# A two-layer hybrid encoder on one core: six weight slots around the projections, splits and copies placed elsewhere

## The reference, cut to what matters

```python
for l in range(2):
    mix = hybrid_mixer(rmsnorm(h, norm_mix_pre[l]), w_in[l], ..., w_out[l])
    h = h + rmsnorm(mix, norm_mix_post[l])
    ff = square(relu(rmsnorm(h, norm_mlp_pre[l]) @ w_mlp_up[l])) @ w_mlp_down[l]
    h = h + rmsnorm(ff, norm_mlp_post[l])
# hybrid_mixer: z = h @ w_in, split into x, gate, q, k, v, g_out, zg
#   RG-LRU group: conv of x, two gated scans (forward, backward), times gelu(gate)
#   GLA group: chunked gated linear attention over q, k, v, both ways, per-head norm, times silu(g_out)
#   concatenate([y_lru, y_gla]) @ w_out
```

## Time and profile before

| | us |
|---|---|
| median of three runs (lowest, highest) | 2449.21 (2448.45, 2449.9) |
| time of the profiled execution | 2447.89 |
| its span, first to last instruction | 2446.1 |
| TensorE busy in the span | 2379.8 |
| GpSimd busy in the span | 751.4 |
| VectorE busy in the span | 1006.9 |

### The profile page before, as it was taken

The page is one execution under the profiler, slowest core; times in us unless marked ns, Lnnn a source line. Parts: engine busy times, 40 slices in busy tenths (PEclk is TensorE's granted clock), DMA queues, the critical chain, the costliest instruction groups (busy, mean ns, idle before and its releaser), DMA issues.

```text
span 2446.1 us, 35177 instructions
## 1 busy us (share of the span) xinstructions
PE 2379.8 (97%) x15144; PEld 2308.1 (94%) x15144; DVE 1006.9 (41%) x989; ACT 585.3 (24%) x719; POOL 751.4 (31%) x401
## 2 busy tenths in 40 slices
PE   7999999999999999999899999999999999999996
PEld 6999989899999999999889998898999999999996
DVE  5688543731221221221577974528221222222226
ACT  4464332321011011011336452414110110110012
POOL 3333213323233233233413421142332332333331
PEclk9999999999999999999999999999999999999998
DMA  3011001511111111111231110015111111111123
GB/s 137 22 56 35 27 27 52 150 52 44 52 43 43 51 43 43 51 60 47 89 113 44 36 43 27 21 63 161 35 53 43 43 51 43 44 50 43 46 76 113
DMA packets 57642, 139.02 MB, mean 57 GB/s; under 512 B 4944, under 2 KB 32848, under 8 KB 57552
## 3 DMA queue, kind: packets, MB, share of 16 engines
q1 hardware_dynamic: 28368, 99.20, 12.4%
q10 hardware_dynamic: 29184, 38.49, 5.0%
HBM read 120.57 MB, written 17.10 MB: 56 GB/s over the span
## 4 chain that ended last, share of the span: by engine, by line
PE 90%; DVE 5%; ACT 2%; issue 1%; POOL 1%; DMA 0%; ACTq 0%; DVEq 0%; SPq 0%; POOLq 0%
PE banks L416 78%; PE banks L517 2%; PE banks L460 2%; DVE Y L1181 1%; PE banks L449 1%; DVE acc L1134 1%; PE banks L450 1%; PE banks L463 1%; PE banks L662 1%; PE banks L669 1%; PE banks L618 1%; PE banks L639 1%; POOL w_hl L348 1%; DVE Y L1191 1%; PE banks L740 1%
## 5 line engine op out<-in xcount | busy, mean ns | idle before, releaser
L416 PE MATMUL banks<-X,w_hl 128*128 128x348 f32 (+1 forms) x7776 | 1263.0, 323 | 6.7 <-POOL w_hl L348 4.8
L416 PEld LDWEIGHTS banks<-X,w_hl 128*128 128x128 f32 x7776 | 1237.9, 188 | 16.1 <-issue 13.2
L346 POOL TENSOR_SCALAR w_hl<-w_raw 128x1024 fp32r<-128x1024 f32 x176 | 200.7, 1140 | 1559.7 <-PE banks L416 1109.9
L416 PE MATMUL banks<-act_hi,w_hl 128*128 128x348 f32 (+1 forms) x2880 | 537.2, 321 | 0.0
L348 POOL TENSOR_TENSOR w_hl<-w_raw,w_hl 128x1024 fp32r<-128x1024 f32 x176 | 497.5, 2827 | 14.7
L416 PEld LDWEIGHTS banks<-act_hi,w_hl 128*128 128x128 f32 x2880 | 471.2, 188 | 0.0
L1080 ACT ACTIVATE T<-T 128x1044 f32<-128x1044 f32 x64 | 69.1, 1079 | 1196.5 <-DVE T L1526 1196.5
L1526 DVE SCALAR_TENSOR_TENSOR T<-banks,rs 128x1044 f32<-128x1044 f32 x64 | 79.7, 1245 | 583.8 <-PE banks L416 573.6
L416 PE MATMUL banks<-act_lo,w_hl 128*128 128x348 f32 (+1 forms) x1440 | 306.4, 321 | 0.0
L1547 DVE TENSOR_TENSOR Y<-banks,Y 128x1044 f32<-128x1044 f32 x96 | 119.5, 1245 | 374.4 <-PE banks L416 374.4
L416 PEld LDWEIGHTS banks<-act_lo,w_hl 128*128 128x128 f32 x1440 | 241.3, 188 | 0.0
(11 more groups left out here) (159 smaller groups left out, 1836.4 us busy)
## 6 DMA issues: line engine op xcount, KB each, us to landing
w_raw<-w_units SPq DMA_DIRECT2D x184, 512.0 KB, 3.4
h_mid<-Y ACTq DMA_DIRECT2D x24, 348.0 KB, 4.2
h_out<-Y ACTq DMA_DIRECT2D x24, 348.0 KB, 2.5
Y<-x_in ACTq DMA_DIRECT2D x6, 696.0 KB, 9.8
h_old<-x_in ACTq DMA_DIRECT2D x12, 348.0 KB, 3.7
h_old<-h_mid ACTq DMA_DIRECT2D x12, 348.0 KB, 3.5
h_old<-h_out ACTq DMA_DIRECT2D x12, 348.0 KB, 3.6
X<-h_mid ACTq DMA_DIRECT2D x6, 696.0 KB, 9.2
```

Of the source, the lines that this page charges most:

```text
L346: nc.gpsimd.tensor_scalar(slot[:, 0], w_raw[:, s], 1.0, 1.0, ALU.mult, ALU.mult).then_inc(w_rounded, 1)
L416: ins = nc.tensor.matmul(out[:, b, 0:width(b)], wp, xp[:, used(b)], start=first and n == 0, stop=last and n == 2)
```

## The change

There are two more slots, 4 and 5 (w_out0 and w_out1), laid over the tiles of gg (A_YL), which are also those of act_hi. The units around the projections go to other slots and are split at other points of GpSimd's order:

- The first pair of each layer goes to slots 0 and 1 instead of 3 and 2. In layer 1 its second unit is split only after the squares of block 0 have been added (acc_done). The layer's units 2 and 3 are split after the jobs of gate 0 and x 0 rather than at once, and the first gate weights between them without a wait for x 0.
- U_OUT+2 and +3 go to slots 4 and 5, after the last `lru_lo` (x_lo) and J_SG[3]; +4 and +5 to slots 0 and 1, +6 and +7 to slots 2 and 3, all after J_O+1.
- U_MLP and U_MLP+1 go to slots 4 and 5 after J_O+2 and J_O+3; U_MLP+2 after J_O+4; U_MLP+3 after J_O+5 and the end of the update (x_lo).
- The last two down units go to slots 2 and 3, with no slot to wait for.
- ScalarE copies v rows 0 and 1 before `decay_exps(0)`, and the later copies are shifted by one; in `update` the norm's `log_mean` and `inv_root` of block 2 stand before `new_piece(5)` instead of after it.

```diff
--- before.py
+++ after.py
@@ -195,6 +195,7 @@
         h_old = at("h_old", [128, 3, 2, BN], A_D)
         w_third = at("w_third", [128, 2, 8, 128], A_D + 2, f32r)
         w_fourth = at("w_fourth", [128, 2, 8, 128], A_T + 3, f32r)
+        w_out = [at("w_out0", [128, 2, 8, 128], A_YL, f32r), at("w_out1", [128, 2, 8, 128], A_YL + 2, f32r)]
         late_sq = (T[0], at("late_sq", [128, NP], A_END))
         sq = at("sq", [128, SQ_RING, 2, BN], A_T + 1)
         Y = at("Y", [128, KT, NP], A_QK)
@@ -202,7 +203,7 @@
         act_lo = at("act_lo", [128, GT, NP], A_SG, f32r)
         assert 4 * 2 * 4 * 128 <= TB and 4 * NC * HEADS * DV <= 5 * TB and 4 * NC * 4 * DV <= 5 * TB
-        wslots = (w_hl[:, 0], w_hl[:, 1], w_third, w_fourth)
+        wslots = (w_hl[:, 0], w_hl[:, 1], w_third, w_fourth, *w_out)
         banks = ctx.enter_context(nc.psum_tensor("banks", [128, 8, 512], f32))
@@ -351,6 +352,11 @@
                 for s, before in ((0, before0), (1, before1)):
                     split(l, i, s, before, wslots[slots[s]])
+            def ups(l, g):
+                i0 = U_MLP // 2 + 4 * g
+                split_pair(l, i0, done(l, j_down(g - 1, 5)), done(l, j_down(g - 1, 7)))
+                split_pair(l, i0 + 1, done(l, j_up(g, 0)), done(l, j_up(g, 1)))
             def downs(l, g, before0, before1):
                 i0 = U_MLP // 2 + 4 * g
                 split_pair(l, i0 + 2, before0, before1)
@@ -359,7 +365,7 @@
             def split_gates(l, t):
                 pool.wait_ge(gatew_loaded, 16 * (l * LT + t + 1))
-                pool.wait_ge(mm_done, FIRST + done(l, j_lru(t - 1, 3) if t > 0 else j_x(0)))
+                pool.wait_ge(mm_done, FIRST + (done(l, j_lru(t - 1, 3)) if t > 0 else l * NJ))
                 pool.sem_inc(waited_pool, 1)
                 nc.gpsimd.tensor_scalar(gates_hl[:, 0], gates_raw[:, :, :], 1.0, 1.0, ALU.mult, ALU.mult).then_inc(gates_hi, 1)
                 pool.wait_ge(gates_hi, l * LT + t + 1)
@@ -368,17 +374,21 @@
             for l in range(L):
-                free = done(l - 1, j_up(0, 1)) if l > 0 else 0
-                split_pair(l, 0, free, free, (3, 2))
+                if l > 0:
+                    split(l, 0, 0, done(l - 1, j_down(GROUPS - 1, 1)), wslots[0])
+                    pool.wait_ge(acc_done, count(ADDS, l - 1, 1) + KT - 1)
+                    split(l, 0, 1, done(l - 1, j_down(GROUPS - 1, 3)), wslots[1])
+                else:
+                    split_pair(l, 0, 0, 0)
                 pool.wait_ge(zgw_loaded, 16 * (l + 1))
                 pool.sem_inc(waited_pool, 1)
                 nc.gpsimd.tensor_scalar(zg_hl[:, :, 0], zg_raw[:, :, :], 1.0, 1.0, ALU.mult, ALU.mult).then_inc(zgw_step, 1)
                 pool.wait_ge(zgw_step, l + 1)
                 nc.gpsimd.tensor_tensor(zg_hl[:, :, 1], zg_raw[:, :, :], zg_hl[:, :, 0].bitcast(f32), ALU.subtract)\
                     .then_inc(zgw_ready, 1)
-                split(l, 1, 0, l * NJ, wslots[1])
-                split(l, 1, 1, l * NJ, wslots[0])
+                split(l, 1, 0, done(l, j_gate(0)), wslots[1])
                 split_gates(l, 0)
+                split(l, 1, 1, done(l, j_x(0)), wslots[0])
                 split(l, 2, 0, done(l, j_v(0)), wslots[1])
                 split_gates(l, 1)
                 split(l, 2, 1, done(l, j_x(1)), wslots[0])
@@ -395,16 +405,23 @@
                 split_pair(l, 8, done(l, J_K[0]), done(l, J_K[1]), (1, 0))
                 split_pair(l, 9, done(l, J_SG[0]), done(l, J_SG[1]), (1, 0))
                 split_pair(l, U_OUT // 2, done(l, J_SG[2]), done(l, J_SG[3]), (1, 0))
-                with pool.Fori(1, 4) as i:
-                    split_pair(l, U_OUT // 2 + i, done(l, J_O - 2 + 2 * i), done(l, J_O - 1 + 2 * i), (1, 0))
-                split_pair(l, U_MLP // 2, done(l, J_O + 1), done(l, J_O + 1), (3, 2))
-                split_pair(l, U_MLP // 2 + 1, done(l, J_O + 7), done(l, J_O + 7))
+                pool.wait_ge(x_lo, l * X_PER + NX + LT)
+                split_pair(l, U_OUT // 2 + 1, done(l, J_SG[3]), done(l, J_SG[3]), (4, 5))
+                split_pair(l, U_OUT // 2 + 2, done(l, J_O + 1), done(l, J_O))
+                split_pair(l, U_OUT // 2 + 3, done(l, J_O + 1), done(l, J_O + 1), (2, 3))
+                split_pair(l, U_MLP // 2, done(l, J_O + 2), done(l, J_O + 3), (4, 5))
+                split(l, U_MLP // 2 + 1, 0, done(l, J_O + 4), wslots[0])
+                pool.wait_ge(x_lo, l * X_PER + NX + LT + HEADS + NX)
+                split(l, U_MLP // 2 + 1, 1, done(l, J_O + 5), wslots[1])
                 downs(l, 0, done(l, j_up(0, 2)), done(l, j_up(0, 3)))
-                with pool.Fori(1, GROUPS) as g:
-                    i0 = U_MLP // 2 + 4 * g
-                    split_pair(l, i0, done(l, j_down(g - 1, 5)), done(l, j_down(g - 1, 7)))
-                    split_pair(l, i0 + 1, done(l, j_up(g, 0)), done(l, j_up(g, 1)))
+                with pool.Fori(1, GROUPS - 1) as g:
+                    ups(l, g)
                     downs(l, g, done(l, j_up(g, 2)), done(l, j_up(g, 3)))
+                g = GROUPS - 1
+                ups(l, g)
+                split_pair(l, U_MLP // 2 + 4 * g + 2, done(l, j_up(g, 2)), done(l, j_up(g, 3)))
+                split_pair(l, U_MLP // 2 + 4 * g + 3, done(l, J_O + 6), done(l, J_O + 7), (2, 3))
         @block.tensor
@@ -450,17 +467,17 @@
                 nc.tensor.matmul(sum_bank(norm, b), ones[:, :], sq[:, n % SQ_RING, 1, :], start=False, stop=last)\
                     .then_inc(sum_done if last else sq_read, 1)
-            def first_pair(l, norm, unit, j, xbase, sbase, last_sum):
+            def first_pair(l, norm, unit, j, slots, xbase, sbase, last_sum):
                 def hi_passes(u, b, k):
-                    w = wslot((3, 2)[u], k)
+                    w = wslot(slots[u], k)
                     for n, wp in enumerate(w):
                         nc.tensor.matmul(ps(j + u)[:, b, 0:width(b)], wp, xtile(k)[0][:, used(b)], start=k == 0 and n == 0, stop=False)
                 def lo_pass(u, b, k):
-                    return nc.tensor.matmul(ps(j + u)[:, b, 0:width(b)], wslot((3, 2)[u], k)[0], xtile(k)[1][:, used(b)],
+                    return nc.tensor.matmul(ps(j + u)[:, b, 0:width(b)], wslot(slots[u], k)[0], xtile(k)[1][:, used(b)],
                                             start=False, stop=k == KT - 1)
                 for n in range(NX):
@@ -729,7 +746,7 @@
             for l in range(L):
                 xbase = l * X_PER
-                first_pair(l, PRE_MIX, 0, j_x(0), xbase, l * 2 * NX, (l - 1, 1, NB - 1) if l > 0 else None)
+                first_pair(l, PRE_MIX, 0, j_x(0), (0, 1), xbase, l * 2 * NX, (l - 1, 1, NB - 1) if l > 0 else None)
                 pe.wait_ge(zgw_ready, l + 1)
                 take_set(l, J_ZG)
@@ -755,12 +772,11 @@
                 unit_with(l, U_K, J_K[0], {3 + n: [rows[n]] for n in range(5)})
                 unit_with(l, U_K + 1, J_K[1], {n: [rows[5 + n]] for n in range(7)})
                 gla(l, xbase)
-                with pe.Fori(1, 3) as i:
-                    unit_job(l, U_OUT + 2 * i, 1, J_O, J_O // 2 + i)
-                    unit_job(l, U_OUT + 2 * i + 1, 0, J_O + 1, (J_O + 1) // 2 + i)
-                by_blocks(l, 0, (U_OUT + 6, U_OUT + 7), (1, 0), [xtile(k) for k in range(KT)], {(1, 0, 5): 0, (2, 1, 6): 1})
-                first_pair(l, PRE_MLP, U_MLP, J_MLP, xbase + NX + LT + HEADS, l * 2 * NX + NX, (l, 0, NB - 1))
+                for m, s in ((2, 4), (3, 5), (4, 0), (5, 1)):
+                    unit_job(l, U_OUT + m, s, J_O + m, (J_O + m) // 2)
+                by_blocks(l, 0, (U_OUT + 6, U_OUT + 7), (2, 3), [xtile(k) for k in range(KT)], {(1, 0, 5): 0, (2, 1, 6): 1})
+                first_pair(l, PRE_MLP, U_MLP, J_MLP, (4, 5), xbase + NX + LT + HEADS, l * 2 * NX + NX, (l, 0, NB - 1))
                 unit_job(l, U_MLP + 2, 0, J_MLP + 2, (J_MLP + 2) // 2)
                 unit_job(l, U_MLP + 3, 1, J_MLP + 3, (J_MLP + 3) // 2)
                 for i in range(4):
@@ -775,7 +791,7 @@
                     unit_job(l, U_MLP + 8 * g + i, i % 2, j_up(g, i), j_up(g, i) // 2)
                 for i in range(2):
                     down_unit(l, g, i)
-                by_blocks(l, 1, (U_MLP + 8 * g + 6, U_MLP + 8 * g + 7), (0, 1), [(act_hi[:, k, :], act_lo[:, k, :]) for k in range(GT)],
+                by_blocks(l, 1, (U_MLP + 8 * g + 6, U_MLP + 8 * g + 7), (2, 3), [(act_hi[:, k, :], act_lo[:, k, :]) for k in range(GT)],
                           {(1, 1, 2): 0, (2, 3, 2): 1})
                 if l == L - 1:
                     row_sum(l, 1, NB - 1)
@@ -877,9 +893,9 @@
                         new_piece(n)
                 else:
                     new_piece(4)
-                    new_piece(5)
                     log_mean(l, norm, 2)
                     inv_root(l, norm, 2)
+                    new_piece(5)
                     new_piece(6)
                     log_mean(l, norm + 1, 0)
                     for n in range(7, NX - 1):
@@ -978,12 +994,13 @@
```

(7 more changed lines are left out.)

## The result

| | before | after |
|---|---|---|
| median, us | 2449.49 (4 runs, 2448.45 to 2449.9) | 2414.76 (4 runs, 2413.53 to 2415.16) |
| profiled execution, us | 2447.89 | 2414.39 |
| its span, us | 2446.1 | 2412.6 |

The median before now has a fourth run in it. The ratio is 0.9862, 95% interval 0.985 to 0.9874: 34.7 us less. The forecast was 2419 with a range from 2411 to 2431.

The account below looks back on a forecast made before the run. TensorE, busy 2379.8 of 2446.1 us, bounds the kernel, so only its waits can be won: ceiling 38.1 us with the clock, less 1.3, 1.4, 3.7 and 1.7, gives 30.0. Forecast 2419 us, range 2411 to 2431.

Parts of the forecast that it names:

- v rows: ScalarE's v copies ahead of the exponentials: TensorE's wait goes, 5.6 us less 1.3, gain 4.3.
- The 0.65 us that it kept for group 8: v rows: TensorE wants group 8 at about 252.0, group 6's copy ends about 252.6; 0.65 us lost per layer.
- Output projection: U_OUT+2 split in front: 8.5 us of waits and clock won, 1.4 lost at head 0; gain 7.1.
- The hidden 0.16: At each listed wait of TensorE: the recorded wait hides 0.16 us more; 17 waits, 2.7 us.
- The head wait of 0.7: Low part of head 0: GpSimd's second subtraction delays the normalisation, a new TensorE wait of 0.7 us per layer.
- The second rival: Head chain at the output projection: turns cost more, 6.3 us a layer instead of 0.7, 2430; chance 0.15.
- by_blocks and first_pair after the mixer: Unit waits in by_blocks, mixer row sums and waits inside first_pair go; two layers gain 9.6 us.
- The reading of the 1.6 us: Inside first_pair: wait follows from VectorE's scalings held by splits of U_MLP+2 and +3; ScalarE's earlier log_mean helps.
- Between the layers: Start of layer 1: TensorE still waits 3.4 us in two parts, slow stretch of 1.7 stays; 5.4 kept in all.
- the hold of VectorE: Between the layers: layer 1's second unit's split and zg make VectorE's scaling wait 1.4 us, its adds 1.3.
- The wait of 1.1 us at the row sum of block 1: Between the layers: a TensorE wait of 1.1 us, beside about 2.3 for the last emptying.
- Layer start: GpSimd's splits beside the convolution delay it 7.5 or 9 us, under the 11 in hand: costs nothing.

Follow-up runs that it names:

- e1_v_old: Changed kernel with only ScalarE's v row copies put back behind the first exponentials; 2421.0 us, ratio 0.9886.
- experiment 2: Four kernels around the 1.6 us first_pair wait: ScalarE's log_mean order and GpSimd's MLP splits undone singly and together, the former alone on the kernel before; 2414.26, 2415.03, 2420.32, 2445.01 us.
- e5_head_free: Changed kernel with U_OUT+3 split only after the last low part of a head; 2413.81 us, ratio 0.9859.
- e3_split_back: Changed kernel with U_MLP+2 and +3 split together behind J_O+7, as before; 2415.03 us, ratio 0.9863.
- e10: Changed kernel with VectorE emptying the last two parts of by_blocks before new_piece(2), between the layers only; 2415.43 us, ratio 0.9865.
- e12: Changed kernel with U_OUT+3 split later, no squares wait, and, between the layers, banks emptied and ScalarE's log_mean and inv_root moved before new_piece(2); 2409.66 us, ratio 0.9841.
- e15_before_log: Kernel before with only log_mean and inv_root of block 2 moved ahead of new_piece(5) on ScalarE; 2445.01 us, ratio 0.9986.
- e4_out_late: Changed kernel with U_OUT+2 and +3 still in slots 4 and 5 but split only after J_O and J_O+1; 2419.12 us, ratio 0.9881.
- e2: Changed kernel with only log_mean and inv_root of block 2 back behind new_piece(5) on ScalarE; 2414.26 us, ratio 0.9857.
- e9: Changed kernel with both ScalarE's log_mean order and the splits of U_MLP+2 and +3 put back as before; 2420.32 us, ratio 0.9884.
- e14: The changed kernel once more, unedited, on the same chip in five rounds; 2414.26 us, ratio 0.9858.
- e6_no_acc_wait: Changed kernel without GpSimd's wait for block 0's squares ahead of layer 1's second unit; 2412.26 us, ratio 0.9852.
- e13_two_waits: Changed kernel with U_OUT+3 split behind the heads and no wait for the squares before layer 1's second unit; 2411.41 us, ratio 0.9849.

## Why the prediction was right, and where it was off

**Sign, size and places** held: 34.7 us measured, 30 forecast, and nearly every wait went or came where the prediction had put it. The forecast lay 4.2 us above the median, which is in its range but 0.2 us under the band, 2415 to 2424, to which it gave most of its chance. Of the miss 3.5 us are in the steps; the rest is that the changed kernel's profiled execution lay only 0.4 below its median, where the prediction had added the 1.3 of the kernel before. Its terms, in its own order:

- **v rows.** The mechanism held: e1_v_old brings the 5.3 us back. The 0.65 us that it kept for group 8 was 0.25 in each layer. VectorE's products were held as it said (two took 5.36 us from 244.33), but the copies of groups 6 to 8 started at 250.70, so group 6's end, put at 252.6, came at 251.3.
- **Output projection.** The waits went and the clock stayed up. Of each step of 4.0 us 2.4 are the wait and 1.6 the clock, where 2.55 and 1.7 were forecast. The hidden 0.16 was not won here, since the changed kernel too takes 0.32 us from start to start where it goes over to U_OUT+2. The clock's part is a dozen matmuls that start 0.29 us apart, from 389.07 on, and 0.16 in the changed kernel. The head wait of 0.7 came as 0.4. The second rival, 6.3 us a layer, did not come: U_OUT+3's raw unit was there, and the second subtraction ended at 366.36.
- **by_blocks and first_pair after the mixer.** 9.6 forecast, 10.1 measured; the last units gave 4.7 and not 4.2. The reading of the 1.6 us was incomplete: it named VectorE as the cause and ScalarE's order as a help, and experiment 2 shows that the wait needs both of them, so that changing either is enough. The other reading would have given the same forecast, so the total could not tell: here the number was right without the mechanism being known.
- **Between the layers.** Measured 5.6, forecast 4.8. The term that was mis-sized is the hold of VectorE: 1.2 us at the scaling and 0.5 at the additions, where 1.4 and 1.3 were forecast. The wait of 1.1 us at the row sum of block 1 did not come: TensorE asked at 1199.01 and the squares had been added at 1198.74. The whole shortage showed at the bank set, 2.3 us as forecast, with its slow stretch, as forecast.
- **Layer start.** "Nothing" held for the time, and here the rows decide what was left open. The convolution in layer 0, VectorE, then GpSimd:

```profile
54.44 2.94 DVE L1332 TENSOR_SCALAR xc<-xb,par 128x1044 f32<-128x1044 f32 x1
57.42 5.80 DVE L1336 SCALAR_TENSOR_TENSOR xc<-xb,par,xc 128x1044 f32<-128x1044 f32 x3
63.26 2.78 DVE L1343 CAST xc_hl<-xc 128x1044 fp32r<-128x1044 f32 x1
```

```profile
54.43 2.40 POOL L349 TENSOR_TENSOR w_hl<-w_raw,w_hl 128x1024 fp32r<-128x1024 f32 x1
57.95 2.17 POOL L372 TENSOR_TENSOR gates_hl<-gates_raw,gates_hl 128x512 fp32r<-128x512 f32 x1
62.21 3.26 POOL L349 TENSOR_TENSOR w_hl<-w_raw,w_hl 128x1024 fp32r<-128x1024 f32 x1
```

In the trace before, the same three lines took 0.81, 3.99 and 0.70 us. The first and the last have one operand in SBUF, and both wait for GpSimd's subtraction as those with two do. By this the rule that the prediction cited from the Trainium skill (GPSIMD Engine Reference, 1. Specifications), that VectorE's two-port modes contend too, agrees with the trace; in which mode the two lines ran, no row here shows. The split's end moved from 62.1 to 67.3, 6.0 us more work between its start and its end against 7.5 to 9 forecast, and TensorE reads it at 72.3: of 11 us in hand 5 are left.

- **The kernel's start** was no term at all, and gave 0.82 us: the clock first rose at 18.6 us and not at 20.4. In the kernels made from the changed one, none of which edits that place, the curve behind it stands at -1.0 us (e5_head_free) to +1.1 (e3_split_back) against the changed kernel, so this part belongs to the execution and is luck.

Of the 3.5 us by which the steps beat the sum, 0.9 are the v rows, 0.6 the head, 0.8 the place between the layers, 0.8 the start, 0.5 the last units, 0.4 first_pair and the rest small; the start of U_OUT+2 takes 0.5 back.

## What to carry to other kernels

Split weights on GpSimd where VectorE is not on the chain that TensorE waits for, and where it can't be avoided, ask how much that chain has in hand. A wait whose chain leaves an in-order engine by two exits (here the bank set and the bank of the sums) may need both moved: one of them alone only moved the wait on (e10), and with both it went (e12). And a wait that two edits each cure tells nothing of its cause until each is undone alone, and then both together. Where the matmuls are the same, the difference of start times by index prices every place in one look.

## What the runs showed of the hardware

- **A wait does not fix the clock.** Waits of 2.1 to 2.6 us in the same place are followed in some executions by 3.4 us at 1.2 GHz (once by 6.8) and in others not; a stretch of 3.4 us cost 1.5 to 1.6 us. Behind the v rows (2.6 us) the clock stayed in both layers of the kernel before, fell in both of e1_v_old and in layer 0 alone of e15_before_log. Behind U_OUT+2 it fell in both layers of the kernel before and stayed in e4_out_late and e15_before_log. Behind the row sums after the mixer (2.1 us) it stayed in the kernel before and fell in both layers of e15_before_log, at 448.6 and 1653.5. Between the layers (2.3 or 2.4 us) it fell in the changed kernel and in e1, e2, e4, e9 and e14, and stayed in e3_split_back and e5_head_free, and in e10_banks_first even behind 3.1 us. Where no wait of this size is left, no fall was seen: in e12_best, which waits 0.9 us at most between the start and the last norm, the clock holds 2.4 GHz from its first rise to there. So it does in the profiles of e6_no_acc_wait and e13_two_waits, where 1.7 us is the longest. What decides it in one execution is not shown here. The first rise, too, belongs to the execution: it came at 20.4 us in the kernel before and at 18.5 in e15_before_log, which is the same there, and at 16.6 to 20.0 in the others. The Trainium skill (TensorE: Matmul & The Clock Gate, Part 1: The HAM clock gate) says of the slow matmuls at a kernel's start that their number is run-variable for one and the same kernel, and the spread of the first rise agrees. So the clock's part of a forecast is a chance, and two profiles that differ by 1 or 2 us at such a place need not differ by their code.
- **Turn-taking works both ways.** GpSimd's rounding took 2.04 us at 60.09 beside VectorE's taps, and 1.05 elsewhere. VectorE's instructions that take one operand from PSUM were not held in the rows seen: L1132 at 53.28 took 1.24 us beside a rounding, and L1173 at 1188.75 took 0.52 beside a subtraction, as they do alone.
